# More seven-product pairs in the feed-forward part, and two of their four weight sums made by adding transfers

## The chip, the core and the metric

The kernel runs on one core of one Trainium2 chip. The metric is the device time of one execution in microseconds (us). Five engines work side by side: TensorE (PE; its weight loads are listed as PEld), VectorE (DVE), ScalarE (ACT), GpSimd (POOL) and SyncE (SP). SP and GpSimd are used here nearly only to issue transfers between HBM and SBUF. Each engine runs its instructions in order and waits for the others by semaphores.

## What is computed

Two layers of a first block and one layer of a second block, on 512 tokens of width 1024. The change touches only the feed-forward half of a layer of the first block (and semaphores at the start of the program):

```
for l in range(DEPTH):                       # DEPTH = 2
    ...
    x = x + jnp.concatenate([y_a, y_b, y_c], axis=-1) @ w_out[l]
    h = rmsnorm(x, ffn_norm[l])
    u = h @ ffn_w_up[l]                      # 512 x 1024 times 1024 x 5632
    a, bv = u[..., :D_FF], u[..., D_FF:]     # D_FF = 2816: gate and value
    a = causal_dwconv(a, ffn_conv_w[l], ffn_conv_b[l])
    x = x + (jax.nn.silu(a) * bv) @ ffn_w_down[l]
```

## The kernel before

Products in full precision are made of three products in a rounded format: every operand is kept as a high part (ScalarE, a copy) and a low part (VectorE, raw minus high), and TensorE adds high x high, low x high and high x low.

**Pairs.** The 2816 gate and 2816 value columns are worked off in 22 pairs, f = 0 to 21 (`KF`): 128 gate columns and 128 value columns with the same number. The weights of a pair are one 1 MB chunk in `w_raw[:, slot]`, with slot f % 2, k = 0 to 7 blocks of 128 rows; columns 0 to 127 are the gate's, 128 to 255 the value's. A plain pair (`up_tile`, L1358 on) is 2 tiles x 8 k x 3 = 48 matmuls of 512 columns. A fast pair (`fast_pair`) takes the pair as a 2 x 2 block product (gate or value; k 0 to 3 or 4 to 7; tokens 0 to 255 or 256 to 511) and makes it of seven products in place of eight, each 4 k x 3 matmuls of 256 columns: 84 matmuls. `PLAIN_F` says which pairs are plain: 0, 1, 2, 4, 8, 12, 16, 20, 21; the other 13 are fast. The seven products need sums of activation blocks (`t_hi`, `t_lo`, made once a layer) and sums of weight blocks, made for each fast pair by VectorE in `weight_sums` (L2523 to L2540): `s_raw[:, 0]` = gate low k + gate high k, `s_raw[:, 1]` = that + value low k, the raw block itself becomes gate low k + value low k, and `s_raw[:, 2]` = `s_raw[:, 1]` + value high k. The sums are then split like weights: `sums_high` on ScalarE (`s_hi`), `sums_low` on VectorE (`s_lo`).

**Order.** No scheduler; each engine's order is written out. In the turn for f (the loop `for f in range(3, KF + 1)`), while TensorE works on pair f:
- ScalarE: `next_up_high(f)` (high part of the weights of f + 1, after the sums of f + 1 are made, since one of them overwrites `w_raw`), then `keep` 1 to 4 (partial results of the running fast pair out of PSUM: to `hid`, to PSUM, to `hid`, to `c_sum`), between them `conv_start(f - 1)` and `sums_high(f + 1)`; at the end `conv_silu(f - 1)`.
- VectorE: gate of f - 1 (`gate_fast` or `gate_tile`, into `a_pad`) and `value_fast(f - 1)`; `split_low` of the weights of f + 1 (`w_lo`, L2155); the taps of the convolution (`conv_taps`, L2505); `sums_low(f + 1)`; `weight_sums(f + 2)`; `first_gate(f)` (L2484); `hidden(f - 1)` (`hid`, L2512), which multiplies gate and value and so frees the value's PSUM bank. The taps stand before or after the sums, by the kind of the pair.
- SP: the weights of f after `split_low(f - 2)` has freed the slot, two transfers of 512 KB, in a loop over f.
- GpSimd: nothing in this stage; earlier in the layer it issues the 16 transfers of `rot_l`.
- TensorE waits in a fast pair f, ahead of its second product, for `hidden(f - 2)` where f - 2 is plain, and for `value_fast(f - 2)` where it is fast; and for the split sums (`s_split`).

## Time and profile before

| | us |
|---|---|
| median of three runs | 1958.09 |
| lowest and highest | 1958.04, 1959.72 |
| the profiled execution | 1960.36 |
| its span, first to last instruction | 1958.60 |
| granted TensorE clock, mean share of full speed | 0.997 |

The span is what the trace covers; the profiled execution took 1.76 us more than it. "Busy" leaves out waits and the issuing of transfers. A row of the timeline gives start, duration, engine, line and operation, output and inputs, how many were merged, and in brackets the idle time before it with what ended it. The start of each row of TensorE is a good clock for its progress; a matmul's printed duration overlaps the next one's start. A row of the windows gives a stretch (from:to), its length, the busy us of PE, PEld, DVE, ACT and POOL with their instructions, then TensorE's granted clock, the DMA engines' mean busy share and GB/s.

### The profile page before, as it was taken

The numbers are of one execution on the slowest core, as the hardware profiler recorded it, in microseconds if no ns is written. First come the engines' busy times: TensorE is split into PE (matmuls) and PEld (weight loads), VectorE is DVE, ScalarE is ACT, GpSimd is POOL, SyncE is SP. The second block draws the span as 40 slices with busy tenths as digits, with TensorE's granted clock in tenths as the row PEclk, the third lists the DMA queues.
The fourth block names the chain that finished last, engine by engine and source line by source line (L and its number), as shares of the span: only waits on it lengthen the run. The fifth ranks groups of instructions, "written<-read, shape, count | busy, mean of one in ns | idle before, by whom it ended". The sixth has DMA issues, their size and how long they took to land.

```text
span 1958.6 us, 31543 instructions
## 1 busy us (share of the span) xinstructions
PE 1928.6 (98%) x11898; PEld 1637.3 (84%) x11898; DVE 1290.1 (66%) x1610; ACT 918.2 (47%) x1401; POOL 30.1 (2%) x60
## 2 busy tenths in 40 slices
PE   7999999999999999999999999999999999999998
PEld 5897889998887897889998888997777777888888
DVE  6866788887645866788887646846664644534435
ACT  5345454555323445455545322344445666544343
POOL 2001000000000001000000000000000000000000
PEclk8999999999999999999999999999999999999999
DMA  7213133333324223133333223533332122232322
GB/s 197 77 46 108 44 107 108 93 102 103 102 76 126 67 56 108 44 103 108 93 107 103 96 82 104 167 86 93 86 112 69 59 82 65 86 119 76 99 89 82
DMA packets 241105, 182.79 MB, mean 93 GB/s; under 512 B 12970, under 2 KB 232360, under 8 KB 240574
## 3 DMA queue, kind: packets, MB, share of 16 engines
q1 hardware_dynamic: 238368, 177.37, 30.5%
q0 software_dynamic: 2160, 2.22, 0.6%
q8 instruction: 94, 1.54, 0.3%
q10 hardware_dynamic: 430, 1.23, 0.2%
q14 instruction: 53, 0.43, 0.1%
HBM read 168.21 MB, written 2.10 MB: 87 GB/s over the span
## 4 chain that ended last, share of the span: by engine, by line
PE 87%; DVE 8%; issue 3%; ACT 2%; DMA 0%; DVEq 0%; ACTq 0%; SPq 0%; POOL 0%
PE ps L882 19%; PE ps L884 18%; PE ps L883 18%; PE ps L1433 4%; PE ps L1432 4%; PE ps L1431 4%; PE ps L669 2%; PE ps L645 2%; PE ps L658 2%; DVE amat L2269 2%; PE ps L1319 1%; PE ps L1318 1%; PE ps L1317 1%; PE ps L521 1%; PE ps L490 1%
## 5 line engine op out<-in xcount | busy, mean ns | idle before, releaser
L882 PE MATMUL ps<-h_hi,w_hi 128*128 128x512 f32 (+1 forms) x1168 | 444.4, 380 | 0.8 <-ACT qk L1636 0.4
L884 PE MATMUL ps<-h_hi,w_lo 128*128 128x512 f32 (+1 forms) x1168 | 434.8, 372 | 0.0
L883 PE MATMUL ps<-h_lo,w_hi 128*128 128x512 f32 (+1 forms) x1168 | 432.7, 371 | 0.0
L2155 DVE TENSOR_TENSOR w_lo<-w_raw,w_hi 128x2048 fp32r<-128x2048 f32 (+3 forms) x110 | 226.9, 2063 | 145.3 <-ACT w_hi L1643 139.6
L1643 ACT ACTIVATE w_hi<-w_raw 128x2048 fp32r<-128x2048 f32 (+3 forms) x108 | 186.9, 1730 | 240.7 <-PE ps L1433 122.0
L882 PEld LDWEIGHTS ps<-h_hi,w_hi 128*128 128x128 f32 x1168 | 219.5, 188 | 43.5 <-issue 6.1
L884 PEld LDWEIGHTS ps<-h_hi,w_lo 128*128 128x128 f32 x1168 | 219.4, 188 | 39.4
L883 PEld LDWEIGHTS ps<-h_lo,w_hi 128*128 128x128 f32 x1168 | 219.6, 188 | 38.9 <-issue 1.9
L2671 DVE TENSOR_TENSOR w_lo<-w_raw,w_hi 128x1024 fp32r<-128x1024 f32 (+1 forms) x118 | 126.5, 1113 | 156.2 <-ACT w_hi L1982 155.4
L882 PE MATMUL ps<-w_hi,h_hi 128*128 128x256 f32 x544 | 152.4, 280 | 0.4 <-DVE h_lo L856 0.4
L883 PE MATMUL ps<-w_lo,h_hi 128*128 128x256 f32 x544 | 150.7, 277 | 0.0
L884 PE MATMUL ps<-w_hi,h_lo 128*128 128x256 f32 x544 | 150.7, 277 | 0.0
L1433 PE MATMUL ps<-hid_hi,w_lo 128*128 128x512 f32 x352 | 138.7, 394 | 0.0
L1432 PE MATMUL ps<-hid_lo,w_hi 128*128 128x512 f32 x352 | 138.0, 392 | 0.0
L1431 PE MATMUL ps<-hid_hi,w_hi 128*128 128x512 f32 x352 | 136.6, 388 | 0.0
L1982 ACT ACTIVATE w_hi<-w_raw 128x1024 fp32r<-128x1024 f32 (+1 forms) x118 | 108.3, 965 | 4.1 <-issue 2.2
L882 PEld LDWEIGHTS ps<-w_hi,h_hi 128*128 128x128 f32 x544 | 102.4, 188 | 1.9 <-DVE h_lo L856 0.8
L883 PEld LDWEIGHTS ps<-w_lo,h_hi 128*128 128x128 f32 x544 | 102.3, 188 | 0.1
L884 PEld LDWEIGHTS ps<-w_hi,h_lo 128*128 128x128 f32 x544 | 102.1, 188 | 0.0
L1432 PEld LDWEIGHTS ps<-hid_lo,w_hi 128*128 128x128 f32 x352 | 66.1, 188 | 15.5
L1431 PEld LDWEIGHTS ps<-hid_hi,w_hi 128*128 128x128 f32 x352 | 66.1, 188 | 14.8
L1433 PEld LDWEIGHTS ps<-hid_hi,w_lo 128*128 128x128 f32 x352 | 66.2, 188 | 13.1
(437 smaller groups left out, 3738.6 us busy)
## 6 DMA issues: line engine op xcount, KB each, us to landing
w_raw<-in_ffn_w_up_dram SPq DMA_DIRECT2D x88, 512.0 KB, 5.0
w_raw<-in_w_in_dram SPq DMA_DIRECT2D x41, 1024.0 KB, 5.3
w_raw<-in_w_in_dram SPq DMA_DIRECT2D x32, 512.0 KB, 5.1
w_raw<-in_ffn_w_down_dram SPq DMA_DIRECT2D x32, 512.0 KB, 4.3
w_raw<-in_w_out_dram SPq DMA_DIRECT2D x12, 1024.0 KB, 5.1
w_raw<-in_ffn_w_down_dram SPq DMA_DIRECT2D x16, 384.0 KB, 3.7
swapped<-qk SPq DMA_DIRECT2D x96, 64.0 KB, 2.0
w_raw<-in_w_mem_kv_dram SPq DMA_DIRECT2D x4, 1024.0 KB, 5.0
```

Of the source, the lines that this page charges most:

```text
L645: ins = pe.matmul(ps[:, b, c:c + n], lhs, rhs, start=first, stop=last)
L658: ins = pe.transpose(ps[:, T_BANK + c // 512, c % 512:c % 512 + P], probs[:, e, c:c + P], ident)
L882: pe.matmul(dst, lh, rh, start=first and j == 0, stop=False, skip_group_check=read_open)
L883: pe.matmul(dst, lh, rl, start=False, stop=False, skip_group_check=read_open)
L884: ins = pe.matmul(dst, ll, rh, start=False, stop=last and j == len(order) - 1, skip_group_check=read_open)
L1431: pe.matmul(dst, wh[:, k, c], hid_hi[:, h, :], start=h == 0, stop=False)
L1432: pe.matmul(dst, wh[:, k, c], hid_lo[:, h, :], start=False, stop=False)
L1433: ins = pe.matmul(dst, wl[:, k, c], hid_hi[:, h, :], start=False, stop=h == KF - 1)
L1643: act.activation(w_hi[:, slot, 0:n], w_raw[:, slot, 0:n], ACT.Copy).then_inc(sem("w_high"), 1)
L1982: act.activation(w_hi[:, slot, q * n:q * n + n], w_raw[:, slot, q * n:q * n + n], ACT.Copy).then_inc(sem("w_high"), 1)
L2155: dve.tensor_tensor(w_lo[:, slot, 0:n], w_raw[:, slot, 0:n], w_hi[:, slot, 0:n].bitcast(F32), ALU.subtract).then_inc(sem("w_split"), 1)
L2671: ins = dve.tensor_tensor(w_lo[:, slot, q * n:q * n + n], w_raw[:, slot, q * n:q * n + n], w_hi[:, slot, q * n:q * n + n].bitcast(F32), AL ...
```

## The change

- `PLAIN_F` becomes 0, 1, 2, 8, 14, 20, 21: 15 of 22 pairs are fast, in runs of five (3 to 7, 9 to 13, 15 to 19).
- Two of the four weight sums leave VectorE. The first (`s_first`; for even f it is `s_raw[:, 0]`, for odd f a new tile) is loaded plainly with the gate's low k on SP's queue, 256 KB, and GpSimd's queue then adds the gate's high k from HBM onto it (`accum_op`). The third (gate low k + value low k) is made by another adding transfer of 256 KB straight onto `w_raw`. The first add waits only for its own plain load, the second for the raw weights. ScalarE, VectorE and the later sums wait for both on `sums_landed0` or `sums_landed1`.
- The two sums left stand behind `hidden(f - 1)` in VectorE's turn.
- The sums are split as one and two (`0, 1` and `1, 3`) where it was two and one. TensorE asks for the second part one product earlier.
- `c_sum` has one buffer where it had two, so `keep` 4 waits for the `first_gate` of the fast pair before. SP's loop over f is written out. Semaphores at the start of the program are merged.

```diff
-PLAIN_F = (0, 1, 2, 4, 8, 12, 16, 20, 21)
+PLAIN_F = (0, 1, 2, 8, 14, 20, 21)
...
+        s_first = [s_raw[:, 0], at("s_first", 92.25, [P, 4, P])[:]]
...
+                for f in range(KF):
+                    s = f % 2
+                    sp.wait_ge(sem("w_split"), upto(sp, "w_split", C_UP + f - 1))
+                    for half in range(2):
+                        sp.dma_start(slot_view(w_raw, s, KD)[:, :, half * P:half * P + P],
+                                     wsrc("ffn_w_up", l, f * P + half * FF, P)).then_inc(sem(f"w_loaded{s}"), 16)
+                    if f in FAST_NO:
+                        if f - 2 in FAST_NO or f - 4 in FAST_NO:
+                            sp.wait_ge(sem("s_split"), upto(sp, "s_split", 2 * FAST_NO[f - 2 if f - 2 in FAST_NO else f - 4] + 1))
+                        sp.dma_start(s_first[s], wsrc("ffn_w_up", l, f * P, P, 0, 4)).then_inc(sem(f"first_loaded{s}"), 16)
...
+                for f in FAST_F:
+                    s = f % 2
+                    up = lambda k0, c0: A["ffn_w_up"][l:l + 1, k0 * P:(k0 + 4) * P, c0:c0 + P].rearrange("a (k p) n -> p (a k) n", p=P)
+                    pool.wait_ge(sem(f"first_loaded{s}"), upto(pool, f"first_loaded{s}", sums_landed(f) // 2))
+                    pool.dma_start(s_first[s], up(4, f * P), accum_op=ALU.add).then_inc(sem(f"sums_landed{s}"), 16)
+                    pool.wait_ge(sem(f"w_loaded{s}"), upto(pool, f"w_loaded{s}", up_loaded(f)))
+                    pool.dma_start(slot_view(w_raw, s, KD)[:, 0:4, 0:P], up(0, FF + f * P), accum_op=ALU.add).then_inc(
+                        sem(f"sums_landed{s}"), 16)
...
                     kept(1)
+                    pe.wait_ge(sem("s_split"), upto(pe, "s_split", 2 * n + 2))
                     product(pe, chain, summed(1), mixed_t(1), range(4), first=False, last=False, read_open=True).then_inc(sem("part_done"), 1)
                     kept(2)
-                    pe.wait_ge(sem("s_split"), upto(pe, "s_split", 2 * n + 2))
...
                     if f + 1 in FAST_NO:
-                        act.wait_ge(sem("s_sum"), upto(act, "s_sum", 4 * FAST_NO[f + 1] + 4))
+                        act.wait_ge(sem(f"sums_landed{(f + 1) % 2}"), upto(act, f"sums_landed{(f + 1) % 2}", sums_landed(f + 1)))
...
                         if f + 1 in FAST_NO:
-                            sums_high(f + 1, 0, 2)
-                            sums_high(f + 1, 2, 3)
-                        keep(f, 4, 5, c_sum[:, s], chain)
+                            sums_high(f + 1, 0, 1)
+                            sums_high(f + 1, 1, 3)
+                        if FAST_NO[f]:
+                            act.wait_ge(sem("fast_sum"), upto(act, "fast_sum", 2 * FAST_NO[f] - 1))
+                        keep(f, 4, 5, c_sum[:], chain)
...
-                    dve.wait_ge(sem(f"w_loaded{s}"), upto(dve, f"w_loaded{s}", loaded))
+
+                    dve.wait_ge(sem(f"sums_landed{s}"), upto(dve, f"sums_landed{s}", sums_landed(f)))
                     if n:
                         dve.wait_ge(sem("s_split"), upto(dve, "s_split", 2 * n))
-                    dve.tensor_tensor(s_raw[:, 0], raw[:, 0:4, 0:P], raw[:, 4:8, 0:P], ALU.add).then_inc(sem("s_sum"), 1)
-                    summed(1)
-                    dve.tensor_tensor(s_raw[:, 1], s_raw[:, 0], raw[:, 0:4, P:2 * P], ALU.add).then_inc(sem("s_sum"), 1)
-                    dve.tensor_tensor(raw[:, 0:4, 0:P], raw[:, 0:4, 0:P], raw[:, 0:4, P:2 * P], ALU.add).then_inc(sem("s_sum"), 1)
-                    summed(2)
+                    dve.tensor_tensor(s_raw[:, 1], s_first[s], raw[:, 0:4, P:2 * P], ALU.add).then_inc(sem("s_sum"), 1)
+                    dve.wait_ge(sem("s_sum"), upto(dve, "s_sum", 2 * n + 1))
                     dve.tensor_tensor(s_raw[:, 2], s_raw[:, 1], raw[:, 4:8, P:2 * P], ALU.add).then_inc(sem("s_sum"), 1)
...
                     if f + 1 in FAST_NO:
-                        sums_low(f + 1, 0, 2)
-                        sums_low(f + 1, 2, 3)
-                    if f + 2 in FAST_NO:
-                        weight_sums(f + 2)
+                        sums_low(f + 1, 0, 1)
+                        sums_low(f + 1, 1, 3)
                     if f in FAST_NO:
                         first_gate(f)
...
                         hidden(f - 1, plain((f - 1) % 2))
+                    if f + 2 in FAST_NO:
+                        weight_sums(f + 2)
```

VectorE's turn for f = 9, where pair 8 is plain and pairs 9, 10 and 11 are fast (its `hid` is the one that pair 10 waits for), before the change:

```order
L2549 TENSOR_TENSOR s_lo<-s_raw,s_hi 128x1024 [waits part_done]
L2544 REGISTER_ALU
L2548 REGISTER_ALU [waits s_high]
L2549 TENSOR_TENSOR s_lo<-s_raw,s_hi 128x512 [waits part_done]
L2532 REGISTER_ALU
L2535 TENSOR_TENSOR s_raw<-w_raw 128x512 [waits s_split,w_loaded1]
L2530 REGISTER_ALU
L2537 TENSOR_TENSOR s_raw<-s_raw,w_raw 128x512 [waits s_sum]
L2538 TENSOR_TENSOR w_raw<-w_raw 128x4x128
L2530 REGISTER_ALU
L2540 TENSOR_TENSOR s_raw<-s_raw,w_raw 128x512 [waits s_sum]
```

and the same turn after it:

```order
L2572 TENSOR_TENSOR s_lo<-s_raw,s_hi 128x512 [waits part_done]
L2564 REGISTER_ALU
L2570 REGISTER_ALU [waits s_sum,s_high]
L2572 TENSOR_TENSOR s_lo<-s_raw,s_hi 128x1024 [waits part_done]
L2510 REGISTER_ALU
L2511 TENSOR_TENSOR ps<-c_sum,ps 128x256 [waits part_kept]
L2538 REGISTER_ALU [waits silu]
L2539 TENSOR_TENSOR hid<-ps,rms_a 128x512 [waits tile_done]
L2541 REGISTER_ALU
L2555 REGISTER_ALU [waits tile_copied]
L2558 TENSOR_TENSOR s_raw<-s_first,w_raw 128x512 [waits s_split,sums_landed1]
L2559 REGISTER_ALU
```

Before, four sums follow the split ones and `ps<-c_sum,ps` and `hid` come after all of them; now these two come first, and two sums follow.

GpSimd's queue in the feed-forward part of a layer, where it had no instruction before, begins with (and goes on in this way for all 15 fast pairs):

```order
L1130 DMA s_first<-in_ffn_w_up_dram 128x4x128 [waits first_loaded1]
L1132 DMA w_raw<-in_ffn_w_up_dram 128x4x128 [waits w_loaded1]
L1130 DMA s_raw<-in_ffn_w_up_dram 128x4x128 [waits first_loaded0]
L1132 DMA w_raw<-in_ffn_w_up_dram 128x4x128 [waits w_loaded0]
L1130 DMA s_first<-in_ffn_w_up_dram 128x4x128 [waits first_loaded1]
```

The two kinds alternate strictly, so the add onto the raw weights of a pair stands behind the wait for that pair's plain load.

## Rows read from the trace of the kernel before

**Rows 1.** The page: busy time, and the chain that ended last.

```profile
PE 1928.6 (98%) x11898; PEld 1637.3 (84%) x11898; DVE 1290.1 (66%) x1610; ACT 918.2 (47%) x1401; POOL 30.1 (2%) x60
...
PE 87%; DVE 8%; issue 3%; ACT 2%; DMA 0%; DVEq 0%; ACTq 0%; SPq 0%; POOL 0%
```

**Rows 2.** Windows by group of four pairs, columns as said above.

```profile
301.45:342.83 41.38, 40.53 (x302) 38.35 (x301) 35.88 (x44) 21.56 (x30) 0.00 (x0) 1.00 0.37 102
...
sum 331.52, PE 324.53 PEld 306.89 DVE 282.88 ACT 172.55 POOL 0.00; mean PE 40.57 PEld 38.36 DVE 35.36 ACT 21.57 POOL 0.00
```

**Rows 3.** Windows of one group by pair, 8 (plain), 9, 10, 11.

```profile
342.83:353.82 10.99, 10.99 (x51) 9.02 (x49) 9.37 (x12) 4.52 (x5) 0.00 (x0) 1.00 0.35 98
353.82:363.57 9.75, 9.75 (x85) 9.75 (x84) 8.17 (x9) 6.34 (x10) 0.00 (x0) 1.00 0.38 104
363.57:374.67 11.10, 10.22 (x86) 9.88 (x85) 10.03 (x14) 6.14 (x9) 0.00 (x0) 1.00 0.35 97
374.67:384.43 9.76, 9.76 (x86) 9.76 (x85) 8.47 (x11) 4.56 (x7) 0.00 (x0) 1.00 0.38 112
```

**Rows 4.** Timeline of TensorE at pair 10, and TensorE's group by form.

```profile
365.98 0.38 PE L882 MATMUL ps<-t_hi,s_hi 128*128 128x256 f32 x1 [0.88 <-DVE hid L2512]
...
L882 PE MATMUL ps<-t_hi,s_hi 128*128 128x256 f32 x208 | 59.8, 288 | 7.0 <-DVE hid L2512 7.0
```

**Rows 5.** Timeline of VectorE, its turn for f = 9.

```profile
355.04 0.69 DVE L2478 TENSOR_TENSOR a_pad<-ps,rms_f 128x512 f32<-128x512 f32 x1
356.32 2.29 DVE L2155 TENSOR_TENSOR w_lo<-w_raw,w_hi 128x2048 fp32r<-128x2048 f32 x1 [0.59 <-ACT w_hi L1643]
...
362.29 0.69 DVE L2535 TENSOR_TENSOR s_raw<-w_raw 128x512 f32<-128x512 f32 x1
363.02 0.69 DVE L2537 TENSOR_TENSOR s_raw<-s_raw,w_raw 128x512 f32<-128x512 f32 x1
363.62 0.68 DVE L2538 TENSOR_TENSOR w_raw<-w_raw 128x512 f32<-128x512 f32 x1
364.23 0.69 DVE L2540 TENSOR_TENSOR s_raw<-s_raw,w_raw 128x512 f32<-128x512 f32 x1
364.83 0.42 DVE L2484 TENSOR_TENSOR ps<-c_sum,ps 128x256 f32<-128x256 f32 x1
365.16 0.68 DVE L2512 TENSOR_TENSOR hid<-ps,rms_a 128x512 f32<-128x512 f32 x1
365.98 0.69 DVE L2492 SCALAR_TENSOR_TENSOR a_pad<-ps,rms_f 128x512 f32<-128x512 f32 x1
```

**Rows 6.** Splitting of the sums, ns min/median/max of both forms.

```profile
L1868 ACT ACTIVATE s_hi<-s_raw x52: 612/837/1063, 286.4 to 1042.1; 128x1024 fp32r<-128x1024 f32 x26, 128x512 fp32r<-128x512 f32 x26
L2549 DVE TENSOR_TENSOR s_lo<-s_raw,s_hi x52: 683/952/1228, 290.5 to 1043.9; 128x1024 fp32r<-128x1024 f32 x26, 128x512 fp32r<-128x512 f32 x26
```

**Rows 7.** SP: timeline, DMA view of 347 to 357, waits of 300 to 500.

```profile
347.68 1.01 SPq L1034 DMA_DIRECT2D w_raw<-in_ffn_w_up_dram  x2
...
q1 hardware_dynamic: 2080, 1.05, 37.4%
...
w_raw<-in_ffn_w_up_dram SPq DMA_DIRECT2D x2, 512.0 KB, 4.8
...
SPq L1034 <- DVE w_lo L2155: 133.2, 15, 9.8
```

**Rows 8.** GpSimd: timeline, landing of `q_stack`, DMA view of 1545 to 1549.

```profile
17.37 1.42 POOL L1106 DMA_DIRECT2D g<-in_b_merge_dram  x1
146.61 7.68 POOL L1117 DMA_DIRECT2D rot_l<-lin  x16 [125.72 <-ACT qr L1636]
...
DMA to landing us min/median/max: 2.2/2.5/4.4
...
g<-in_b_merge_dram POOLq DMA_DIRECT2D x1, 12.0 KB, 7.1
...
q0 software_dynamic: 160, 0.26, 34.0%
```

102 lines of the change are left out of this document (55 added, 47 removed).

## The prediction

> **What bounds the kernel now.** I read the page first. TensorE is busy 98% of the span and holds 87% of the chain that ended last [rows 1]; in the stretches of interest its granted clock is 1.00 [rows 2]. So the time is TensorE's own work plus its few waits. The change touches the first product of the feed-forward part (once in each of two layers), so I then cut that stretch into groups of four pairs. A group, one plain pair and three fast ones, takes 41.4 to 41.6 us [rows 2, 3], and the eight groups of both layers (f = 4 to 19, twice) take 331.52 us [rows 2]. One cut by pair shows the inside of a group: 10.99 us for the plain pair, 9.75 and 9.76 us for two fast pairs, and 11.10 us for the fast pair that comes second after the plain one, where TensorE is busy only 10.22 us [rows 3]. That one waits 0.88 us for the gating product `hid` of VectorE; it is the only wait inside the groups worth a name, and the row that groups it over the program has 7.0 us of it [rows 4], eight pairs.
>
> **Step 1, two more fast pairs a layer.** A plain pair is 48 products of 512 columns, a fast one 84 of 256 columns; a pair's turn falls from 10.99 to 9.76 us, 1.23 us each [rows 3]. Fast go 4, 12 and 16, plain goes 14. In f = 4 to 19 of both layers there are now 8 plain and 24 fast pairs, and after the change 4 plain and 28 fast.
>
> **Step 2, the wait.** Where pair f-2 is plain and f-1 fast, pair f needs the bank that `hidden(f-2)` frees. In VectorE's turn for the pair before, that instruction stands behind the four weight sums. The turn that holds it goes from `a_pad` at 355.04 to the next `a_pad` at 365.98 us: 10.94 us against TensorE's 9.75 [rows 5]. `hid` starts at 365.16 and ends 0.68 later, 365.84, and TensorE starts its next product at 365.98. Unhindered, TensorE would have come there at 363.57 + 1.36 (12 products of the 9.76 us / 84) = 364.96, so the wait is worth about 1 us plus the uneven restart. After the change the sums stand behind `hidden`; without them, it ends 365.84 - 2.54 (362.29 to 364.83 for the four) = 363.3 us, 1.7 us before TensorE needs it. Next in line for TensorE are then the split of the next weights (done at 358.5, needed 363.6) and the two split sums; none is late.
>
> **Sum on TensorE.** 28 x 9.76 + 4 x 10.99 = 317.2 us in place of 331.5: 14.3 us less. Of this 4 x 1.23 = 4.9 us come from step 1 and the rest from step 2 (8 waits of some 1.1 to 1.3 us with what they drag). This holds only if each fast pair can go on at 9.76 us, five in a row, which the other engines must keep up with.
>
> **Step 3, VectorE's turn.** Two adds leave it, from `s_raw<-w_raw` at 362.29 to the next at 363.02 and the `w_raw` add from 363.62 to 364.23: 0.73 + 0.61 = 1.34 us, so 10.94 becomes 9.6 us [rows 5]. That turn includes 0.59 us of waiting for ScalarE's `w_hi`. The cut of the split sums moves against it. Before, ScalarE and VectorE split two sums and then one; now one and then two. The second part may start only when the fourth product of the pair has read the old one, about 5.8 us into the pair (359.6), and is now the long one: 1.06 us on ScalarE and then 1.23 on VectorE, where before the short ones of 0.61 and 0.68 stood [rows 6]. That ends 0.9 us later at most, of which 0.3 was already a wait. I reckon the turn by its fixed point, since the split of the weights can't start before ScalarE's copy, 2.3 to 2.5 us into a pair: from there split 2.2, taps 1.6, first sum 0.7, then the second part ends near 8.1, `ps` and `hid` at 9.1, two sums at 10.5, gate and value of the next pair at 11.7, and the next split may start at 9.76 + 2.3 = 12.1. So VectorE keeps up with 0.4 us to spare. That is thin, but it has several us of slack against TensorE's own needs, so only a turn that is longer on the average costs anything. I charge nothing and keep the bound: 0.25 us too much in each of 28 pairs costs 7 us.
>
> **Step 4, the transfers.** Each fast pair gets three more transfers of 256 KB: a plain one on SP's queue, behind the two of the raw weights, and two adding ones on GpSimd's. SP is no bottleneck: it stood waiting for VectorE for 133.2 us of one stretch of 200, and its pair of issues takes 1.01 us [rows 7]. The plain load waits for the first split sum of the pair two before; queued behind it on SP is the next pair's load, due 7.8 us later. GpSimd waits for nothing else in that stage, and nothing but the rotated copies of the next layer stands behind it. Issuing costs 0.48 us for a transfer of 16 pieces of 2 KB (7.68 / 16) and 1.42 us for one of 128 x 24 pieces [rows 8]; I take 0.9 us for each adding transfer, its 512 pieces lying between. From issue to landing a 128 KB transfer of that queue takes 2.5 us, with 2.2 to 7.1 at the ends [rows 8].
>
> No row shows an adding transfer. The bounds of its engine time come from two rows: the raw weights' 1.05 MB took 37.4% of 10 us on the 16 DMA engines, 3.74 us, so 256 KB copied in 512-byte pieces is 0.94 us [rows 7]; and 0.26 MB moved inside SBUF by GpSimd's queue took 34.0% of 4 us, 1.36 us [rows 8]. Below is a plain copy, 0.94; above I put twice the slower one, 2.7, for reading both operands. I take 1.9, twice the copy of the same pieces. An end of 2.7 changes nothing, as follows.
>
> (The Trainium skill, Collectives: The Full Stack, section "The bandwidth ceiling: the fold count and why AG ≠ RS ≠ AR", says that an adding transfer is slow not for the arithmetic but since it must read two sources where a copy reads one, measured 1.93 to 1. By that rule it is 1.8 us. The Trainium skill's DMA: Bandwidth & Descriptors, section Anatomy of one DMA, prices a transfer of this queue at 2.0 us and the bytes at 436 GB/s, which would give 2.6 us from issue to landing for the transfer, as if adding were free. Neither moves the sum; the first speaks for a small chance of the third rival. No row of this trace shows either.)
>
> Time line, from the start of pair f-2 (weights for pair f+1): the split that frees the slot ends at 4.5, the raw weights are issued at 4.9 and landed 4.8 later [rows 7], 9.7. The first half is issued at 6.9 (after the split sum of step 3), moves behind them (0.94 us and a margin) and is there by 10.8. The first add takes 1.9 us of moving in place of `q_stack`'s 1.36 for two transfers, so I put 3.5 from issue to landing: 14.3. The second follows it on the same engines, 1.9 later and a little: 16.3. VectorE wants both at 18.9, ScalarE at 19.8. So 2.5 us are to spare, and 0.7 with 2.7 us each. The chain from split to landing may last 14.7 us before it sets the pace (two turns of 9.76, less sums, gate and split, 4.8); it lasts 11.8.
> The engines' load: six pairs in a stretch (five fast, one plain) last 5 x 9.76 + 10.99 = 59.8 us and move 6 x 3.74 + 5 x 0.94 + 10 x 1.9 = 46.1 us of DMA work. They saturate when an add costs (59.8 - 27.1) / 10 = 3.3 us, and the whole gain (14.3 / 6 = 2.4 us for each of the six stretches) is gone at 3.5.
>
> **Forecast.** Span 1958.60 - 14.3 = 1944.3 us; around it lie 1.76 us (the profiled execution took 1960.36), and the profiled one stands 2.27 above the median of 1958.09. So 1943.8 us in the median, 0.7% faster. The merged start semaphores and SP's unrolled loop cost nothing: the waits stay the same, and SP idles.
>
> **Rivals.**
> (a) VectorE falls short: the second split part, the sums and their semaphore waits make its turn 10.0 instead of 9.6 to 9.75. For it speaks the 0.4 us of slack; against it that the turn of 355 to 366 us holds 0.89 us of waits that it can eat. 1943.8 + 7 = 1951.
> (b) The adds reach the edge, 3.5 us each or a landing a few us later, and TensorE gives back what it gained: within 0.2%, 1958. For it: nothing of this kind was ever seen here. Against: the 2.7 bound.
> (c) Slower: the DMA engines saturate. If an adding transfer reads, adds and writes piece by piece and costs four times a copy, 3.74 us, the six pairs need 27.1 + 37.4 = 64.5 us of DMA, 4.7 more than TensorE; six such stretches add 28 us: 1972. It decides from 3.5 us an add, and each 0.1 us more costs 6 us. For it: the small 512-byte pieces, and the mix with SP's queue. Against: DMA now stands at 0.37 of the stretch [rows 2], so nearly two thirds are free.
>
> **Chances.** Forecast 0.63, (a) 0.14, (b) 0.06, (c) 0.17. What a measurement of this kernel can tell is about 0.2%, 3.9 us: below 1954.2 is faster, above 1962.0 slower. So faster 0.77, same 0.06, slower 0.17. The range goes from 1941.5 (the first fast pairs gain a little more) to 1960, over (a) and (b), and leaves (c) out.
>
> **What would show it.** Right: pairs at 9.76 us five in a row, no wait of a product for `hid`, the two adds landed 3 us before VectorE's sums. Wrong in step 4: VectorE waiting at its first weight sum, or ScalarE at `w_hi`, for a transfer; DMA share of the stretch near 1 instead of 0.77; GpSimd's issues far over 0.9 us. Wrong in step 3: TensorE waiting for `s_lo` or `w_lo` with the transfers long landed, VectorE busy without a gap.

## The result, and the profile after the change

The changed kernel takes 2004.67 us in the median of 4 runs (2002.4 to 2007.63), the kernel before 1958.14 beside it (1958.04 to 1959.72): the ratio is 1.0233, 95% interval 1.022 to 1.0246. That is 46.5 us slower than before and 61 us above the forecast of 1943.8, far outside the range. The profiled execution has a span of 2000.6 us, against 1958.60 before.

The page of the changed kernel, as [rows 1] were of the kernel before: busy times, the queue of GpSimd, the chain that ended last, TensorE's first product of a split sum, and GpSimd's transfers.

```profile
PE 1942.7 (97%) x12042; PEld 1658.3 (83%) x12042; DVE 1275.4 (64%) x1582; ACT 929.4 (46%) x1425; POOL 107.7 (5%) x120
...
q0 software_dynamic: 33840, 17.95, 7.0%
...
PE 74%; DMA 10%; DVE 8%; issue 4%; ACT 2%; POOL 0%; SPq 0%; ACTq 0%; DVEq 0%
...
L887 PE MATMUL ps<-t_hi,s_hi 128*128 128x256 f32 x240 | 73.5, 306 | 36.2 <-ACT hid L1896 35.3
...
w_raw<-in_ffn_w_up_dram POOLq DMA_DIRECT2D x30, 256.0 KB, 6.7
```

TensorE held 87% of the chain before; now it holds 74%, and transfers, which held nothing, hold 10%. The wait for VectorE's `hid` (7.0 us in [rows 4]) is gone; in its place stand 35.3 us of waiting for ScalarE's copy into `hid` (`keep` 1), five times as much. And TensorE is busy 14 us longer (1942.7 against 1928.6), though faster pairs should have made it less: it also ran at a lower clock.

Windows of four fast pairs of the changed kernel, columns as in [rows 2]. After removing the waits of [rows 3] every row should read 9.76.

```profile
300.20:317.80 17.60, 12.11 (x86) 11.91 (x85) 10.35 (x14) 6.05 (x9) 2.56 (x2) 0.81 0.92 188
358.11:372.78 14.67, 11.52 (x85) 11.32 (x84) 8.89 (x11) 6.05 (x9) 2.57 (x2) 0.88 0.90 176
372.78:382.54 9.76, 9.76 (x86) 9.76 (x85) 9.13 (x12) 6.14 (x9) 2.57 (x2) 1.00 0.69 128
392.30:406.89 14.59, 11.52 (x86) 11.32 (x85) 9.05 (x11) 6.05 (x9) 0.00 (x0) 0.88 0.56 135
```

Most pairs do run at 9.76 us, and plain pairs at 10.99, as forecast. But in f = 4 to 19 of the first layer five of the 14 fast pairs take 14.3 to 17.6 us, and the 16 pairs last 186.96 us where the forecast says 158.62. 28.3 us for one layer. The same stretch of the second layer takes 26 us longer than in the fastest kernel below, which is near the forecast: together nearly the whole miss. In the pair at 358.11 some 3.2 us are a wait, and the 11.52 of busy time, where 9.76 would do, come from the clock, 0.88 in the mean.

The timeline around that pair: SyncE's and GpSimd's issues, then ScalarE, VectorE and TensorE.

```profile
342.14 1.07 SPq L1037 DMA_DIRECT2D w_raw<-in_ffn_w_up_dram  x2
343.38 1.76 SPq L1042 DMA_DIRECT2D s_raw<-in_ffn_w_up_dram  x1
352.50 1.01 SPq L1037 DMA_DIRECT2D w_raw<-in_ffn_w_up_dram  x2
...
351.37 1.26 POOL L1130 DMA_DIRECT2D s_raw<-in_ffn_w_up_dram  x1 [9.59 <-DMA s_raw<-in_ffn_w_up_dram]
352.12 1.82 POOL L1132 DMA_DIRECT2D w_raw<-in_ffn_w_up_dram  x1
...
361.91 1.91 ACT L1657 ACTIVATE w_hi<-w_raw 128x2048 fp32r<-128x2048 f32 x1 [5.71 <-DMA w_raw<-in_ffn_w_up_dram]
363.73 0.37 ACT L1896 ACTIVATE hid<-ps 128x256 f32<-128x256 f32 x1
...
361.76 0.69 DVE L2558 TENSOR_TENSOR s_raw<-s_raw,w_raw 128x512 f32<-128x512 f32 x1 [4.67 <-DMA w_raw<-in_ffn_w_up_dram]
...
364.22 0.58 PE L887 MATMUL ps<-t_hi,s_hi 128*128 128x256 f32 x1 [3.15 <-ACT hid L1896]
```

Read it from the end. TensorE waits for `keep` 1. ScalarE makes that copy in 0.37 us, but it stands behind `w_hi`, and ScalarE stood at `w_hi` for 5.71 us waiting for the second adding transfer. GpSimd issued that at 352.12, 10 us after the raw weights were issued (342.14), because it first waited for the plain first half, 8 us on its way (343.38 to 351.37), and it landed only at about 361.7 (352.12 + 9.6), 19.6 us after the raw load was issued. My working had 11.4 (4.9 to 16.3).

Three windows of the DMA view of the same stretch, 352 to 356.5, 356.5 to 358 and 358 to 361.7 (packets, MB, share of 16 engines; q0 is GpSimd's queue, q1 SyncE's), tell why the add took 9.6 us.

```profile
q0 software_dynamic: 527, 0.26, 48.0%
q1 hardware_dynamic: 599, 0.31, 27.8%
...
q1 hardware_dynamic: 972, 0.49, 110.0%
q0 software_dynamic: 3, 0.00, 0.6%
...
q1 hardware_dynamic: 1037, 0.51, 57.5%
q0 software_dynamic: 526, 0.26, 55.7%
```

In the first window the first add's packets move, and SyncE's next raw load (issued 352.50) begins beside them; in the second that load fills the engines; in the third, as it thins out, the second add moves, side by side with the rest of SyncE's packets.

### The profile page after: what moved, and what is told of

Same layout as the page of the kernel before. It is cut to its first block, busy times and chain, and to the rows that moved or that the text cites. A ratio compares the mean times of both kernels' runs of the same rounds, so it can differ in the third digit from the quotient of the medians.

```text
span 2000.6 us, 32051 instructions
## 1 busy us (share of the span) xinstructions
PE 1942.7 (97%) x12042; PEld 1658.3 (83%) x12042; DVE 1275.4 (64%) x1582; ACT 929.4 (46%) x1425; POOL 107.7 (5%) x120
## 3 DMA queue, kind: packets, MB, share of 16 engines
q0 software_dynamic: 33840, 17.95, 7.0%
q10 hardware_dynamic: 430, 1.23, 0.2%
## 4 chain that ended last, share of the span: by engine, by line
PE 74%; DMA 10%; DVE 8%; issue 4%; ACT 2%; POOL 0%; SPq 0%; ACTq 0%; DVEq 0%
PE ps L887 15%; PE ps L889 14%; PE ps L888 14%; DMA w_raw<-in_ffn_w_up_dram 5%; PE ps L1447 4%; PE ps L1446 4%; PE ps L1445 4%; DMA s_first<-in_ffn_w_up_dram 2%; PE ps L674 2%; PE ps L650 2%; PE ps L663 2%; DVE amat L2296 2%; DMA s_raw<-in_ffn_w_up_dram 2%; PE ps L1331 1%; PE ps L1333 1%
## 5 line engine op out<-in xcount | busy, mean ns | idle before, releaser
L887 PE MATMUL ps<-h_hi,w_hi 128*128 128x512 f32 (+1 forms) x1136 | 428.8, 377 | 1.0 <-ACT qk L1650 0.4
L889 PE MATMUL ps<-h_hi,w_lo 128*128 128x512 f32 (+1 forms) x1136 | 418.5, 368 | 0.0
L888 PE MATMUL ps<-h_lo,w_hi 128*128 128x512 f32 (+1 forms) x1136 | 416.5, 367 | 0.0
L887 PEld LDWEIGHTS ps<-h_hi,w_hi 128*128 128x128 f32 x1136 | 213.5, 188 | 41.2 <-issue 6.7
L889 PEld LDWEIGHTS ps<-h_hi,w_lo 128*128 128x128 f32 x1136 | 213.3, 188 | 37.2
L888 PEld LDWEIGHTS ps<-h_lo,w_hi 128*128 128x128 f32 x1136 | 213.6, 188 | 36.0 <-issue 1.9
L887 PE MATMUL ps<-t_hi,s_hi 128*128 128x256 f32 x240 | 73.5, 306 | 36.2 <-ACT hid L1896 35.3
L887 PEld LDWEIGHTS ps<-t_hi,s_hi 128*128 128x128 f32 x240 | 49.7, 207 | 38.8 <-issue 37.5
```

Source lines behind the costliest of these rows:

```text
L887: pe.matmul(dst, lh, rh, start=first and j == 0, stop=False, skip_group_check=read_open)
L888: pe.matmul(dst, lh, rl, start=False, stop=False, skip_group_check=read_open)
L889: ins = pe.matmul(dst, ll, rh, start=False, stop=last and j == len(order) - 1, skip_group_check=read_open)
```

## Experiments

There are sixteen kernels: the first twelve tell which part of the change costs, the last four why. Each was compared with the kernel before on the same chip, and ratios are to that; not all ran on the same chip, so times of two experiments compare less closely than each with the kernel before.

### The adding itself, the runs of five, the order on ScalarE and on GpSimd

The changed kernel with plain copies in place of the adding transfers:

```diff
-                    pool.dma_start(s_first[s], up(4, f * P), accum_op=ALU.add)...
+                    pool.dma_start(s_first[s], up(4, f * P))...
```

(and the same for `w_raw`; both sums then lack one operand).

> The changed kernel with both adding transfers made plain copies of the same bytes on the same queue (the sums are then wrong by the operand that is not added; everything else runs). If the adding itself is what costs (66 ns a piece of 512 bytes against about 30 for a plain piece): engine time of the queue halves, each lands 1 us earlier or more, and the waits mostly go: 1950 to 1965. If it is the row of dependent transfers and the software queue (issue, start, landing) that is too long whatever is in them: 1980 to 2005.

Measured: 1948.83 us, ratio 0.9945 (0.9929 to 0.9962), with pairs at 9.76 us five in a row. The page of that kernel, GpSimd's queue:

```profile
q0 software_dynamic: 6960, 17.95, 3.5%
```

Same bytes, in the same places, but half the engine time (3.5% of the span on 16 engines, of which 0.6 is not theirs: 0.9 us a transfer, against 2.1), 80 packets a transfer against 528 (6960 and 33840 in all), 0.75 us to issue against 1.26 and 1.82, and 3.5 and 3.7 us to land against 4.7 and 6.7. So steps 1 to 3 of the prediction hold in the main, and the adding is what costs. The time is a little under what I expected, and 5 us over the forecast: `w_hi` still waits for a copy three times, 9.4 us in all. Which of the four differences (engine time, packets, issue, landing) matters most, this run doesn't tell.

The changed kernel with the old set of pairs:

```diff
-PLAIN_F = (0, 1, 2, 8, 14, 20, 21)
+PLAIN_F = (0, 1, 2, 4, 8, 12, 16, 20, 21)
```

> The changed kernel with the old set of plain pairs (13 fast pairs a layer in runs of three, as before), all else as changed. Theory P: a plain pair in four gives the chain 1.2 us more and VectorE no third sum to make, so there are fewer waits per pair but still some: 1965 to 1985, above 1958. If only the runs of five are at fault and three in a row can be fed: the four waits a layer for `hid` are gone and nothing new comes, 1958.1 - 9.4 = 1949.

Measured: 2000.95 us, ratio 1.0214 (1.0194 to 1.0234), with 30.2 us of TensorE's wait for ScalarE's `hid`. That is above both ranges of the expectation. Runs of three stall as runs of five do.

The changed kernel with `w_hi` behind `keep` 3 on ScalarE:

```diff
-HIGH_PLACE = {}
+HIGH_PLACE = {f: 3 for f in FAST_F}
```

> The changed kernel with one edit: in a fast pair's turn ScalarE makes the high part of the next weights after keep 3 instead of ahead of keep 1. Theory O (order): in the changed kernel the adds land 2 to 5 us after ScalarE's turn for them comes, and this reaches TensorE only because ScalarE's w_hi stands ahead of keep 1, which TensorE needs 2.8 us into the pair. Then lateness of up to about 4 us is hidden, the ten waits of 3 us for `hid` go, and with them the low clock behind each: 10 x 4.9 = 49 us less than 2004.7, some 1950 to 1960. Theory P (pace): from the split that frees a slot to the landing of the last add 15 to 20 us pass, where two turns leave 14.7, so the stretch of five pairs can't run at 9.76 us whatever ScalarE's order is; the waits only move to TensorE's wait for w_lo or s_lo, and the time stays above 1985.

Measured: 2019.02 us, ratio 1.031 (1.0291 to 1.0329). ScalarE's wait for the add at `w_hi` falls from 64.7 to 4.5 us, yet TensorE still waits 30.2 us for `hid`, in smaller pieces, and the last two pairs of each run of five take 12.1 us. The time is in theory P's range, but in these pairs neither TensorE, VectorE nor ScalarE waits for a transfer. One of them, from 467.24 to 479.35 (VectorE, ScalarE, TensorE):

```profile
469.11 2.29 DVE L2182 TENSOR_TENSOR w_lo<-w_raw,w_hi 128x2048 fp32r<-128x2048 f32 x1 [2.67 <-ACT w_hi L1657]
...
477.99 0.81 ACT L1862 ACTIVATE rms_a<-a_pad,g 128x512 f32<-128x512 f32 x1 [2.16 <-DVE a_pad L2519]
...
479.35 0.38 PE L887 MATMUL ps<-t_hi,w_hi 128*128 128x256 f32 x1 [1.05 <-ACT hid L1896]
```

VectorE stands 2.67 us for the later `w_hi`, so it comes late to `a_pad`; ScalarE waits for that ahead of `keep` 3, and TensorE for `keep` 3. The edit thus brings a circle of waits of its own, and doesn't tell whether a late add could be hidden in this place.

The changed kernel with GpSimd's two adds exchanged (the raw add, with its wait for the raw weights, ahead of the first one):

```diff
-                    pool.wait_ge(sem(f"first_loaded{s}"), upto(pool, f"first_loaded{s}", sums_landed(f) // 2))
-                    pool.dma_start(s_first[s], up(4, f * P), accum_op=ALU.add)...
                     pool.wait_ge(sem(f"w_loaded{s}"), upto(pool, f"w_loaded{s}", up_loaded(f)))
                     pool.dma_start(slot_view(w_raw, s, KD)[:, 0:4, 0:P], up(0, FF + f * P), accum_op=ALU.add)...
+                    pool.wait_ge(sem(f"first_loaded{s}"), upto(pool, f"first_loaded{s}", sums_landed(f) // 2))
+                    pool.dma_start(s_first[s], up(4, f * P), accum_op=ALU.add)...
```

> The changed kernel with GpSimd's two adds of a pair swapped: first the one onto the raw weights (waits for the raw weights), then the one onto the first sum (waits for its plain load). If the plain load of the first half, which lands last on SP's queue, holds up everything behind it (theory Q, queue): the first add starts 1 to 3 us earlier and the pair of adds lands 1 to 3 us earlier, so the five waits of a layer shrink: 1975 to 1990. If the adds themselves and their sharing of the engines with the next raw load set the landing: within 5 us of 2004.7.

Measured: 1975.97 us, ratio 1.0087 (1.0059 to 1.0115), 29 us less than the changed kernel, in theory Q's range. The order matters, but doesn't cure it: `w_hi` waits on a count to which both adds contribute, and now the other add is the late one (waits of the kernel with the adds exchanged; total, times, longest):

```profile
ACT w_hi L1657 <- DMA s_first<-in_ffn_w_up_dram: 29.9, 8, 6.6
ACT w_hi L1657 <- DMA s_raw<-in_ffn_w_up_dram: 21.6, 5, 5.5
```

### The steps without transfers

The kernel before with the new set of pairs only:

```diff
-PLAIN_F = (0, 1, 2, 4, 8, 12, 16, 20, 21)
+PLAIN_F = (0, 1, 2, 8, 14, 20, 21)
```

> The kernel before with the new set of 15 fast pairs and nothing else. Step 1 alone would give 4.9 us, and the waits for `hid` stay where a plain pair stands two before (3 a layer and not 4): 1958.1 - 4.9 - 2.2 = 1951. If VectorE's turn of 10.9 us adds up over five pairs (my reason why two sums had to leave VectorE): 1.1 us more in each of the last pairs of a run, 1960 to 1970.

Measured: 1972.10 us, ratio 1.0065 (1.0048 to 1.0082); in a run of five, pairs take 9.75, 10.89, 10.79, 10.83 and 9.76 us. This is 2 us over the range expected if VectorE's turns add up. VectorE is the wait there (its sums hold `w_hi` for 65.0 us in all): with four sums it can't carry a run of fast pairs at 9.76 us.

The kernel before, with the sums behind `hidden` in the one turn whose `hid` TensorE waits for (f fast, f-1 plain):

```diff
-                    if f + 2 in FAST_NO:
+                    behind = f in FAST_NO and f - 1 not in FAST_NO
+                    if f + 2 in FAST_NO and not behind:
                         weight_sums(f + 2)
...
                         hidden(f - 1, plain((f - 1) % 2))
+                    if f + 2 in FAST_NO and behind:
+                        weight_sums(f + 2)
```

> The kernel before with one edit, no adding transfers: in the turn where f is fast and f - 1 plain (4 a layer) VectorE makes the four weight sums behind `hidden` and not ahead of `first_gate`. My step 2 says that the wait of TensorE for `hid` goes, 8 times about 1.1 us: 1949 to 1951. Rival: the sums now end 1.5 us later, ScalarE's w_hi waits for them ahead of keep 1, and TensorE waits for keep 1 in place of `hid`, some 1 us each: 1957 to 1960.

Measured: 1983.19 us, ratio 1.0117 (1.01 to 1.0134). Its timeline, ScalarE and TensorE in the pair that [rows 3] show with 11.10 us and that now takes 13.87:

```profile
369.68 1.91 ACT L1643 ACTIVATE w_hi<-w_raw 128x2048 fp32r<-128x2048 f32 x1 [4.79 <-DVE s_raw L2540]
...
371.92 0.58 PE L882 MATMUL ps<-t_hi,s_hi 128*128 128x256 f32 x1 [2.45 <-ACT hid L1879]
```

Both ranges of the expectation missed it, the rival's (1957 to 1960) by 23 us, though the rival had the mechanism: `hid` is in time, but the four sums, now later, hold `w_hi`, `w_hi` holds `keep` 1, and a wait of 0.88 us has become one of 2.45 with a lowered clock behind it. It is the changed kernel's stall without any adding transfer: what makes `w_hi` late may be a sum or a DMA.

The kernel before, with the new set, all four sums behind `hidden`, the sum onto the raw weights made second and `w_hi` waiting for no more than that:

```diff
-                    dve.tensor_tensor(s_raw[:, 1], s_raw[:, 0], raw[:, 0:4, P:2 * P], ALU.add)...
                     dve.tensor_tensor(raw[:, 0:4, 0:P], raw[:, 0:4, 0:P], raw[:, 0:4, P:2 * P], ALU.add)...
+                    dve.tensor_tensor(s_raw[:, 1], s_raw[:, 0], raw[:, 0:4, P:2 * P], ALU.add)...
...
-                        act.wait_ge(sem("s_sum"), upto(act, "s_sum", 4 * FAST_NO[f + 1] + 4))
+                        act.wait_ge(sem("s_sum"), upto(act, "s_sum", 4 * FAST_NO[f + 1] + 2))
```

> The kernel before with the new set of 15 fast pairs and all four sums on VectorE, no transfers: the sums stand behind `hidden` in every turn, the one onto the raw weights is made second, and ScalarE's w_hi waits only for the first two. If VectorE can carry four sums in runs of five (about 56.7 us of work in the 59.8 of six pairs, worked out from its 36.0 us in a group of four before): 1944 to 1950. If not (a turn of 10.9 us against 9.76 adds up over five pairs and ScalarE waits for the sums): 1955 to 1970.

Measured: 1970.31 us, ratio 1.006 (1.0043 to 1.0077), most fast pairs at 10.3 to 10.9 us, just above the second range. VectorE's work itself is too long for TensorE's 9.76 us with four sums; sums must leave it.

### One adding transfer instead of two

The changed kernel with the first add only; the third sum is VectorE's again, as the first of three behind `hidden`, and `w_hi` waits for it:

```diff
-                    pool.wait_ge(sem(f"w_loaded{s}"), upto(pool, f"w_loaded{s}", up_loaded(f)))
-                    pool.dma_start(slot_view(w_raw, s, KD)[:, 0:4, 0:P], up(0, FF + f * P), accum_op=ALU.add)...
...
+                    dve.tensor_tensor(raw[:, 0:4, 0:P], raw[:, 0:4, 0:P], raw[:, 0:4, P:2 * P], ALU.add)...
```

> The changed kernel with one adding transfer a pair in place of two: GpSimd's queue makes only the first sum; VectorE makes the third (onto the raw weights) again, as the first of its three, and ScalarE's w_hi waits for that one and no longer for a transfer. Theory C (chain of two adds: the second is issued behind the first, shares the engines with it and with the next raw load, and lands 6.7 us after its issue in the middle, where the first takes 4.7): with the second gone nothing that ScalarE waits for hangs on a landing, and the first lands in time: the ten waits go, 1944 to 1950. Rival: any adding transfer behind the plain load is too late for the turn, whichever it is; VectorE then waits at its second sum, and 1965 to 1985 remains.

Measured: 1951.27 us, ratio 0.9956 (0.9939 to 0.9973): faster than before, no stalls, pairs at 9.76 to 10.03 us. They aren't all at 9.76, since `w_hi` now waits 51.3 us in all for VectorE's sum.

The same with the old set of pairs:

```diff
-PLAIN_F = (0, 1, 2, 8, 14, 20, 21)
+PLAIN_F = (0, 1, 2, 4, 8, 12, 16, 20, 21)
```

> The run with only the first sum by an adding transfer (1951.3 us), with the pairs of the kernel before (13 by seven products a layer, not 15). It tells how much of its 8 us under the kernel before comes from the two more fast pairs a layer and how much from the sum taken off VectorE. Theory (steps 1 and 2 of the prediction add): two more fast pairs a layer are worth 1.23 us each at 9.76 us, less 0.27 us for each of the 15 pairs that VectorE holds at 10.0 us; so the old set gives 1951.3 + 4.9 - 1 to 2 = 1953 to 1956 us. Rival (the runs of five are what costs there, VectorE catching up only in plain pairs): the old set is as fast as the new one or faster, 1948 to 1951.5 us.

Measured: 1950.38 us, ratio 0.9948 (0.9932 to 0.9965). Here the rival was right: two more fast pairs a layer bring nothing in this form, since with the old set TensorE is held for 9.91 us in one pair of three, and with the new one for 9.90 to 10.03 in three of a run of five.

The mirror: the raw add only. VectorE adds the other half onto the plainly loaded first half, in place:

```diff
-                    pool.wait_ge(sem(f"first_loaded{s}"), upto(pool, f"first_loaded{s}", sums_landed(f) // 2))
-                    pool.dma_start(s_first[s], up(4, f * P), accum_op=ALU.add)...
...
+                    dve.tensor_tensor(s_first[s], s_first[s], raw[:, 4:8, 0:P], ALU.add)...
```

> The changed kernel with one of its two adding transfers left: the one onto the raw weights (third sum). The first sum is VectorE's: it adds the other half of the raw weights onto the plainly loaded first half, in place, behind `hidden`, as the first of three sums; the plain load of the first half stays. This is the mirror of the run that kept only the add onto the first half (1951.3 us). Two theories. (A, two adds on one queue) Each add alone is early enough: raw weights landed after 5.5 us, issue 1.8 us, landing at most 6.7 us more with the other add on the way and less without it, together 12 to 14 us where 14.7 are allowed (raw load issued to the first need of the sum). The stall came from the raw add standing on GpSimd's queue behind the wait for the first half's plain load (8 us in the late pairs) and its issue (1.26 us). Then the time is 1950 to 1956 us (fast pairs at 9.8 to 10.0 us, as in the mirror, with VectorE carrying three sums), the granted clock 0.99 or more and TensorE's wait for ScalarE's `hid` under 5 us in all. (B, the raw add itself) An add onto the raw weights is on the way between the raw load and ScalarE's w_hi whatever else is queued, with a landing of 5.5 to 10 us; then stalls of 3 to 5 us with a lowered clock behind them stay in several fast pairs a layer and the time is 1965 to 1985 us, near the 1976 us of the run with the two adds swapped.

Measured: 1944.54 us (1942.83 to 1945.43), ratio 0.9918 (0.9901 to 0.9934). This is the fastest kernel of the study, 0.8% under the kernel before, and the forecast for the changed one to within a microsecond, though with three sums on VectorE. Windows of its run of five, columns as before:

```profile
349.98:359.74 9.76, 9.76 (x86) 9.76 (x84) 8.39 (x11) 6.14 (x9) 1.28 (x1) 1.00 0.72 158
359.74:369.50 9.76, 9.76 (x87) 9.76 (x85) 9.38 (x12) 6.15 (x9) 1.28 (x1) 1.00 0.64 141
369.50:379.26 9.76, 9.76 (x87) 9.76 (x85) 9.17 (x13) 6.14 (x9) 1.29 (x1) 1.00 0.67 148
```

VectorE's turn, by the first of its three sums in three pairs one behind the other, is 10.24 us:

```profile
359.49 0.69 DVE L2555 TENSOR_TENSOR s_first<-s_first,w_raw 128x512 f32<-128x512 f32 x1 [0.21 <-DVE hid L2537]
...
369.73 0.69 DVE L2555 TENSOR_TENSOR s_raw<-s_raw,w_raw 128x512 f32<-128x512 f32 x1 [0.21 <-DVE hid L2537]
...
379.97 0.69 DVE L2555 TENSOR_TENSOR s_first<-s_first,w_raw 128x512 f32<-128x512 f32 x1 [0.21 <-DVE hid L2537]
```

Theory A of its expectation holds in its mechanism, and the time is better than its 1950 to 1956: the raw add stands on the direct path to `w_hi` and is no trouble alone. How much of the 0.8% comes from the two more fast pairs wasn't tested for this form.

The third sum computed by GpSimd itself, ahead of its adding transfer of the first half:

```diff
+                    pool.wait_ge(sem(f"w_loaded{s}"), upto(pool, f"w_loaded{s}", up_loaded(f)))
+                    pool.tensor_tensor(raw[:, 0:4, 0:P], raw[:, 0:4, 0:P], raw[:, 0:4, P:2 * P], ALU.add)...
```

> The changed kernel with the first sum by an adding transfer, and the third sum (128x512, onto the raw weights) computed by GpSimd itself instead of by a transfer: GpSimd waits for the raw weights, adds, and then issues the adding transfer of the first half. Two sums stay on VectorE. No trace here shows such an operation on GpSimd; VectorE takes 0.69 us for it. It has from the raw weights' landing (5.5 us after their issue) until 14.7 us after it, so up to 9 us are allowed. Theory A and B agree that the adding transfer onto the raw weights was at fault, so both say that the stalls go: 1944 to 1949 us (forecast level; fast pairs at 9.76 us, since VectorE has 0.7 us less than in the run with three sums at 10.03 us). The rival: VectorE and GpSimd slow one another down while both work on SBUF, VectorE's operations beside it take measurably longer than 0.69 and 2.28 us, and the time is that of three sums on VectorE or worse, 1951 to 1965 us.

Measured: 1960.74 us, ratio 1.0003 (0.9994 to 1.0013), missed by both theories' 1944 to 1949 and inside the rival's 1951 to 1965. The rival had the mechanism too, in part. GpSimd's sum takes 1.28 us where VectorE leaves it alone and up to 3.36 (median 1.39), and VectorE's `w_lo`, 2.28 or 2.29 us in all 88 cases of the kernel with the raw add alone, takes 2.78 to 3.21 in six. Two overlaps in that kernel, GpSimd and VectorE:

```profile
314.68 1.29 POOL L1131 TENSOR_TENSOR w_raw<-w_raw 128x512 f32<-128x512 f32 x1 [9.35 <-DMA w_raw<-in_ffn_w_up_dram]
314.95 3.17 DVE L2182 TENSOR_TENSOR w_lo<-w_raw,w_hi 128x2048 fp32r<-128x2048 f32 x1
...
366.08 3.36 POOL L1131 TENSOR_TENSOR w_raw<-w_raw 128x512 f32<-128x512 f32 x1 [7.79 <-DMA w_raw<-in_ffn_w_up_dram]
366.00 2.28 DVE L2182 TENSOR_TENSOR w_lo<-w_raw,w_hi 128x2048 fp32r<-128x2048 f32 x1
368.20 2.58 DVE L2532 SCALAR_TENSOR_TENSOR rms_a<-a_pad,g,rms_a 128x512 f32<-128x512 f32 x2
```

Whichever starts second is longer by about the rest of the other, and where GpSimd was second the next operation of VectorE is longer as well (the two taps take 1.53 us elsewhere). And the add of the first half, issued that much later, now comes late for VectorE in 10 pairs (waits of that kernel). How the loss splits between the two wasn't tested.

```profile
DVE s_raw L2559 <- DMA s_first<-in_ffn_w_up_dram: 20.8, 6, 4.8
...
DVE s_raw L2559 <- DMA s_raw<-in_ffn_w_up_dram: 8.8, 4, 3.0
```

The changed kernel with SyncE's plain load of the first half ahead of the raw weights:

```diff
+                    if f in FAST_NO and (f - 2 in FAST_NO or f - 4 in FAST_NO):
+                        sp.wait_ge(sem("s_split"), ...)
+                        sp.dma_start(s_first[s], wsrc("ffn_w_up", l, f * P, P, 0, 4))...
                     sp.wait_ge(sem("w_split"), upto(sp, "w_split", C_UP + f - 1))
                     for half in range(2):
...
-                    if f in FAST_NO:
...
+                    if f in FAST_NO and f - 2 not in FAST_NO and f - 4 not in FAST_NO:
```

> The changed kernel with both adds in their order, but SyncE issues the plain load of the first half (for all fast pairs but the first two of a layer) ahead of the pair's raw weights, not behind them, with its wait for `s_split` ahead too. GpSimd then issues the first add while the raw load is still moving, and the second as soon as the raw weights are there. Theory A (queue order is the fault): the chain from the raw load to the landed second add becomes 5.5 + 1.8 + 5 to 6.7 = 12.3 to 14 us against 19.6 us in the late pairs, so the time falls at least to that of the swapped adds, 1976 us, and to 1950 to 1960 us if nothing else holds. Theory B (an add's transfer is itself too long: 66 ns a piece of 512 B on each engine where a plain one takes about 30): the raw load now shares the engines with the first add and lands later than 5.5 us (7 or more), the second add still lands late in some pairs, and the time stays at 1975 to 2000 us. If SyncE's wait for `s_split`, now ahead of the raw load, holds that load back, the raw load of each fast pair shows it, and the time is above 2000 us.

Measured: 1984.22 us, ratio 1.0112 (1.0078 to 1.0145), theory B's range. The second add is now issued in 1.28 us as soon as the raw weights are there, and still lands after 4.5 to 9.4 us; four pairs of the first layer stall. And something else happened, which the expectation had named: SyncE's wait for the split sum, now ahead, holds the raw load back (VectorE, then SyncE in that kernel):

```profile
361.82 2.28 DVE L2183 TENSOR_TENSOR w_lo<-w_raw,w_hi 128x2048 fp32r<-128x2048 f32 x1
...
366.53 0.37 SPq L1037 DMA_DIRECT2D s_raw<-in_ffn_w_up_dram  x1
367.08 1.00 SPq L1040 DMA_DIRECT2D w_raw<-in_ffn_w_up_dram  x2
```

The slot is free when `w_lo` ends (364.10), and the raw load is issued 3.0 us later; in the changed kernel the median is 0.2 us.

### Why two don't fit

The single raw add, made to meet SyncE's next load, with no transfer more:

```diff
                     pool.wait_ge(sem(f"w_loaded{s}"), upto(pool, f"w_loaded{s}", up_loaded(f)))
+                    pool.wait_ge(sem("w_split"), upto(pool, "w_split", C_UP + f))
```

> The run with the raw add alone (1944.5 us), but GpSimd issues the add of pair f only when the split is done that also lets SyncE issue the raw weights of pair f+1: no transfer is added, the add is made to meet the next burst. Theory G: the add's packets stand behind that burst of 1.25 MB (4 to 5 us), so it lands 8 to 11 us after its issue where it landed after 4.3 to 5.0; it is issued some 10 us after its raw load, is due 14.7 us after it, and so comes 3 to 6 us late in nearly every fast pair: 1990 to 2050 us, with the lowered clock behind the waits. Without such a preference (packets of both queues served side by side) it lands 5 to 6 us after its issue, at most 1.5 us late, which ScalarE's and TensorE's waits partly hide: 1945 to 1970 us.

Measured: 2023.52 us, ratio 1.0325 (1.03 to 1.0349). The landing times of the raw add, first in the kernel with that add alone, then in this one:

```profile
DMA to landing us min/median/max: 4.3/4.6/5.0
```

```profile
DMA to landing us min/median/max: 6.5/7.2/9.0
```

The two ranges don't touch. One add of this kernel, issued at 324.83 us; the DMA view of 325 to 329 and of 329 to 331.5:

```profile
q1 hardware_dynamic: 1755, 0.89, 81.0%
...
q0 software_dynamic: 526, 0.26, 83.8%
q1 hardware_dynamic: 325, 0.16, 24.1%
```

Between 325 and 329 not one of its packets moves (q0 has no line there); it waits until SyncE's burst, a raw load of 1.05 MB issued 0.37 us before it, has nearly passed. The median landing is less than the 8 to 11 us that I expected: a free add also moves none for about 2.2 us (issued 371.52, packets from 373.7 to 376.2 in the kernel with the raw add alone), and that delay overlaps the burst. Packets served side by side, the other theory, would have landed it after 5 to 6 us. Worked out from the packets of all adds: until its eleventh packet starts an add takes 2.1 to 2.3 us in each of the 30 cases of the kernel with the raw add alone, where SyncE's queue is still meanwhile, and 2.7 to 4.7 us (median 4.5) in the 30 of this one, where SyncE's packets fill at least 0.88 of the engines. In the next kernel, with the wait for the first half, both kinds occur side by side: 2.1 to 2.3 us in 25 adds, 3.5 to 4.7 in the five that met a burst. So a burst holds an add's start. Once started, it moves beside SyncE's packets, as the first window of the changed kernel shows. Whether SyncE's packets are preferred or were only first in line, no run tells.

The kernel with the raw add alone, which also waits for the plain first half before it issues:

```diff
                     pool.wait_ge(sem(f"w_loaded{s}"), upto(pool, f"w_loaded{s}", up_loaded(f)))
+                    pool.wait_ge(sem(f"first_loaded{s}"), upto(pool, f"first_loaded{s}", sums_landed(f)))
```

> The run with the raw add alone (1944.5 us), and GpSimd waits for the plain load of the first half too before it issues that add, as in the changed kernel; no transfer is added. Theory G: no change of more than 2 us (1943 to 1948 us), since both loads move in one burst and land within about 1 us of one another, and the add still falls into the gap. Theory Q: if the wait for the first half is what made the raw add late, stalls return: 1960 us or more.

Measured: 1954.66 us, ratio 0.9979 (0.9968 to 0.9989): 10 us more for one wait than the raw add alone, dearer than theory G said, cheaper than Q.

The changed kernel with the first add made a plain copy, and the second an add:

```diff
-                    pool.dma_start(s_first[s], up(4, f * P), accum_op=ALU.add)...
+                    pool.dma_start(s_first[s], up(4, f * P))...
```

> The changed kernel with both of GpSimd's transfers in their order, but the first is a plain copy (its sum lacks one operand; the bytes and the place in the queue stay). It moves in about 1 us of the DMA engines where an add takes 2.1, and costs GpSimd 0.75 us to issue where an add costs 1.26. Theory G (the gap): GpSimd's packets move only in the gap between SyncE's bursts of raw weights; in the run with the raw add alone that gap is some 5 us wide in a turn of 9.76 (burst over at 361.2, next from 366.8 us), the add moves from 364.0 to 366.2, and two adds of 2.1 us, issued one behind the other, don't fit, while a copy and an add (3.1 us) nearly do. So few fast pairs stall: 1944 to 1960 us. Theory Q (the order on GpSimd's queue, the raw add behind the wait for the plainly loaded first half): that order is as in the changed kernel, so 1976 us or more.

Measured: 1973.81 us, ratio 1.008 (1.0063 to 1.0097), between the two theories' ranges, nearer Q.

The first-half load ahead and the adds exchanged, which is the edits of two earlier experiments together:

> The changed kernel with the plain load of the first half issued ahead of the raw weights and, on GpSimd, the raw add ahead of the first add: the shortest chain for the sum that w_hi waits for. Theory G: the raw add is issued as the burst ends and moves in the gap, so w_hi is never late; the first add follows and in some pairs meets the next burst, where it has 4 to 5 us more until it is due (ScalarE's first s_hi). So better than each edit alone (1976 and 1984 us): 1950 to 1972 us, but not as fast as the run with the raw add alone. If it is no better than 1976 us, the room for the first add is used up as well, and two adds don't fit in any order.

Measured: 2010.06 us, ratio 1.0263 (1.0241 to 1.0286), a miss. The two edits help singly and not together: this is no better than the changed kernel. I overlooked two things. `w_hi` waits for both adds, so the order of GpSimd's queue can't shorten its chain; its waits for the first-half add, now the later one, are 93.0 us here. And SyncE's wait for the split sum holds the raw load back by 3.0 us in the median, as in the kernel with the load ahead.

G and Q can be read as one theory: what counts is when the last add that `w_hi` waits for is issued and what it meets. Worked out from the traces of all nine kernels with the new set of pairs, `w_hi` in its place, and `w_hi` waiting for a transfer of GpSimd's (30 fast pairs each), in us from the end of the split that frees the slot to the landing of the last such transfer, which the prediction allows 14.7 and reckoned at 11.8:

| kernel | ahead of the last transfer | median | longest | over 14.7 | time |
|---|---|---|---|---|---|
| raw add alone | nothing | 11.4 | 12.9 | 0 | 1944.5 |
| both plain copies | wait and a copy | 12.6 | 17.2 | 3 | 1948.8 |
| alone, with the wait | wait | 13.4 | 19.0 | 4 | 1954.7 |
| copy, then add | wait and a copy | 15.0 | 18.8 | 20 | 1973.8 |
| adds exchanged | wait and an add | 15.7 | 19.7 | 21 | 1976.0 |
| load ahead | SyncE's wait, an add | 16.0 | 19.7 | 20 | 1984.2 |
| changed kernel | wait and an add | 17.0 | 20.4 | 25 | 2004.7 |
| load ahead, adds exchanged | SyncE's wait, wait and an add | 19.0 | 21.9 | 24 | 2010.1 |
| alone, with the next load | next split | 20.2 | 22.0 | 30 | 2023.5 |

The time follows the median of the chain row by row. The kernel with `w_hi` behind `keep` 3 (14.7 in the median, 2019.0 us) doesn't fit, having a circle of waits of its own. What stands ahead of the add pushes it later by its own length, and towards SyncE's next burst; in the kernel made to meet that burst it lands 6.5 to 9.0 us after its issue in place of 4.3 to 5.0. How each kernel's lateness splits between the two was not worked out.

## Why the prediction was wrong

**Step 1** (1.23 us a pair) holds: 10.99 and 9.76 us are measured wherever nothing is late. But only together with sums taken off VectorE, as the new set in the kernel before (1972.1) shows.

**Step 2** holds in its mechanism: no wait for VectorE's `hid` is left in the changed kernel. Its closing sentence, that nothing else is late next, holds only while `w_hi` is in time; the move of the sums in a single turn of the kernel before made `keep` 1 the next wait, at 2.45 us.

**Step 3** holds. No run shows the two sums of the forecast costing anything: in the kernel with plain copies, which has them, pairs go at 9.76 us five in a row with VectorE busy 9.14 us of them at most. With three sums VectorE starts its turns 10.24 us apart in the fastest kernel; one sum less (0.61 to 0.73 us) makes an estimate of 9.5 to 9.6, the forecast's 9.6, so rival (a)'s 10.0 was too high. Even 10.24 cost nothing there, since the turn without sums at the end of a run of five takes the lag back. What the step left out is ScalarE: its `w_hi` stands ahead of `keep` 1, which TensorE needs for its second product, so a late `w_hi` reaches TensorE as a wait of 1.7 to 5.7 us, ten times in the changed kernel.

**Step 4** is the one that failed, and not by the engine time of an add. The add costs the engines 2.1 us (7.0% of 16 engines' 2000.6 us, less the 0.6% of before, over 60 adds) where I took 1.9; the limit of 14.7 us is about right, as the table shows. Wrong was the chain of 11.8 us from the split to the last landing (11.4 from the issue of the raw load), measured at 17.0 and 16.9 in the median, and over the limit in 25 of 30 pairs:

- The plain first half took 5.9 (odd f) and 7.7 us (even f) to land, not 3.9: 1.05 MB issued just ahead are on the same engines, and in part the adds of the pair before.
- The second add was issued 9.4 us after the raw load, not 6.8.
- It landed 6.7 us later in the median, up to 10.2, not 4.6. I put a fixed time on each transfer, "1.9 later and a little", on engines that another queue was filling. The load I did work out, 77% of the engines; this averages over bursts at 100% and gaps, and an add that comes after the start of a burst moves only as the burst thins out.

Rival (c) had the sign but not the mechanism: an add took 2.1 us of the engines, not 3.74, and they were not saturated. Their mean share in the 16 pairs is 0.70 of 186.96 us, some 131 us of work; in the 158.62 us of the forecast that would be 0.83, more than my 0.77 and still short of 1. The signature that I named for step 4 came out, VectorE waiting 57.4 us at its first sum and ScalarE 64.7 at `w_hi` for transfers (waits of the changed kernel):

```profile
ACT w_hi L1657 <- DMA w_raw<-in_ffn_w_up_dram: 64.7, 12, 7.9
DVE s_raw L2558 <- DMA w_raw<-in_ffn_w_up_dram: 57.4, 17, 5.5
```

And no step priced the clock. In the changed kernel TensorE's granted clock fell to the lower of its levels (1.2 GHz) at nine of its ten waits for `hid` of more than 1 us; by the busy time beyond 9.76 this cost 1.76 to 2.80 us in each of the five stalled pairs of the first layer, 30 to 46% of the stall.

Three small slips of the working change nothing in the forecast: 12 products of 9.76 us / 84 are 1.39 us, not 1.36 (the 364.96 is right); the long second parts of the split sums end 1.0 us later than the short ones, not 0.9; and with adds of 2.7 us the time line leaves 1.0 us, not 0.7.

## What to carry to other kernels

Price a transfer on a path by its issue and its landing under the load that is there, burst by burst, not by its bytes and the engines' mean share; ask for each one which burst it meets if it comes 1 us later. Moving work from an engine to a transfer can pay (the kernel with one adding transfer and two more fast pairs a layer is 0.8% faster), but a second one on the same queue, behind one more wait, can cost far more than the first brought. And look for what stands behind the waiting instruction on its in-order engine: here a copy of 0.37 us carried the delay to TensorE.

## What the runs showed of the hardware

- An adding transfer of 256 KB in 512-byte pieces costs GpSimd 1.26 us to issue (1.82 right behind another), a plain one 0.75. It keeps the DMA engines 2.1 us against 0.9, which is about 65 ns a piece against 27 to 33 for SyncE's plain ones. As GpSimd's only transfer in a pair it landed after 4.3 to 5.0 us (median 4.6); the first of two plain copies took 3.3 to 4.1 (median 3.5).
- Issued 0.37 us behind a raw load of SyncE's (1.05 MB), one such transfer moved no packet for 4 us, where one with the engines free moved none for 2.2. Over all 30 adds of each kernel the eleventh packet started 2.7 to 4.7 us after the issue against 2.1 to 2.3, and the landing came after 6.5 to 9.0 us against 4.3 to 5.0.
- GpSimd added 128x512 f32 values in 1.28 us where VectorE takes 0.69. When it overlapped VectorE's split of 128x2048 values (2.29 us alone), the one that started second was longer by about the rest of the other: up to 3.36 us on GpSimd, up to 3.21 on VectorE.
- TensorE's granted clock, 1.00 in every steady pair, was 0.78 to 0.89 in the mean over each of the five pairs of the first layer with a wait of 2.65 us or more in the changed kernel (0.5, the lower of its two levels, in the part behind the wait), and 1.00 again in the next pair. The length of a wait alone doesn't decide: in the kernel with the sums of one turn moved the clock fell at waits of 1.83 us, and in the changed kernel with the old set it stayed at 1.00 over a pair with one of 2.57.
